# TensorE's identity products at three waits of each RWKV pair: loops of one product instead of products written out

## The reference

```python
def rwkv_mixer(pa, s0, w0, w_up, a0, a_up, g_up, k_k, k_a, r_k, gn_g, gn_b):
    ...
    r, k, v, wlo, alo, glo = jnp.split(pa, idx, axis=-1)
    kkf = heads((k * k_k).astype(jnp.float32))
    kk = kkf * lax.rsqrt(jnp.sum(kkf * kkf, axis=-1, keepdims=True) + 1e-12)
    g = jax.nn.sigmoid(glo) @ g_up
    for d, rev in enumerate((False, True)):
        w_log = -jax.nn.softplus(-(w0[d] + jnp.tanh(wlo) @ w_up[d]).astype(jnp.float32)) - 0.5
        decay = jnp.exp(-jnp.exp(w_log))
        a = jax.nn.sigmoid(a0[d] + alo @ a_up[d])
        kd = k * (1 + (a - 1) * k_a)
        y, s_fin = rwkv_scan(heads(r), heads(decay), heads(kd), heads(v), kk, heads(a), s0[:, d], rev)
    ...
```

## Time and profile before

| | |
|---|---|
| median of 3 runs | 3560.22 us (3550.71 to 3563.60) |
| the profiled execution, its own time | 3554.39 us |
| its span from first to last instruction | 3552.7 us |
| TensorE busy, share of the span | 3312.4 us, 93% |
| stage `rwkv` in the span | about 99 to 917 us |
| granted TensorE clock over the span | 0.981 of full speed |

### The profile page before, as it was taken

How to read it: one execution, slowest core, us unless ns; L and a number is a source line. 1 busy time by engine, 2 the same in 40 slices (tenths; PEclk the granted TensorE clock), 3 DMA queues, 4 the chain that set the end, 5 groups by cost and what they waited for, 6 DMA issues and landing times.

```text
span 3552.7 us, 155850 instructions
## 1 busy us (share of the span) xinstructions
PE 3312.4 (93%) x72354; PEld 2871.3 (81%) x72354; DVE 2133.6 (60%) x3890; ACT 765.1 (22%) x1815; POOL 388.7 (11%) x536
## 2 busy tenths in 40 slices
PE   7989899898999999299999999999999999999998
PEld 3575767767455545299999999999999999999997
DVE  4566667575344434666666666666666666666665
ACT  3434344444244443000000000000000000000002
POOL 0141524334211000000000000000000000000001
PEclk9999999999999999699999999999999999999999
DMA  8200000000311113399898898999889989898996
GB/s 358 73 5 9 18 10 17 5 20 5 99 33 33 44 54 107 128 325 286 284 290 278 290 285 281 286 291 287 283 287 288 284 282 292 284 289 287 283 288 211
DMA packets 570775, 671.20 MB, mean 189 GB/s; under 512 B 56942, under 2 KB 463750, under 8 KB 567054
## 3 DMA queue, kind: packets, MB, share of 16 engines
q1 hardware_dynamic: 564430, 641.85, 55.5%
q0 software_dynamic: 5520, 19.34, 2.4%
q10 hardware_dynamic: 176, 0.05, 0.0%
HBM read 631.68 MB, written 28.30 MB: 186 GB/s over the span
## 4 chain that ended last, share of the span: by engine, by line
PE 56%; issue 1%; SPq 1%; DVE 0%; DMA 0%; ACT 0%; DVEq 0%
PE banks L2515 34%; PE banks L2540 21%; PE banks L2456 2%; SPq L2363 1%; SPq L2370 0%; DMA e_wgu<-in_e_up 0%; DVE e_wgu L2819 0%; SPq L2373 0%; DVE e_wgu L2888 0%; DVE e_xe L2877 0%; DVE e_wsum L2717 0%; ACT e_xp L2655 0%; ACT e_xT L2655 0%; DVE e_wgu L2722 0%; DVE e_hid L2769 0%
## 5 line engine op out<-in xcount | busy, mean ns | idle before, releaser
L2540 PE MATMUL banks<-e_hid,e_wd 128*64 128x144 f32 x11264 | 1242.0, 287 | 6.7 <-issue 3.8
L2540 PEld LDWEIGHTS banks<-e_hid,e_wd 128*64 128x64 f32 x11264 | 744.4, 137 | 8.3 <-issue 8.2
L2515 PE MATMUL banks<-e_xsum,e_wsum 128*64 128x72 f32 x11264 | 514.3, 226 | 10.5 <-issue 7.8
L2515 PE MATMUL banks<-e_xT,e_wgu 128*64 128x72 f32 x11264 | 511.7, 226 | 12.6 <-issue 10.3
L2515 PE MATMUL banks<-e_xsum,e_wgu 128*64 128x72 f32 x11264 | 510.9, 226 | 7.9 <-issue 7.8
L2515 PEld LDWEIGHTS banks<-e_xsum,e_wsum 128*64 128x64 f32 x11264 | 492.7, 137 | 13.8 <-issue 11.0
L2515 PEld LDWEIGHTS banks<-e_xT,e_wgu 128*64 128x64 f32 x11264 | 491.4, 137 | 15.1 <-issue 14.8
L2515 PEld LDWEIGHTS banks<-e_xsum,e_wgu 128*64 128x64 f32 x11264 | 489.5, 137 | 10.1 <-issue 10.0
L2750 DVE TENSOR_TENSOR e_gu<-e_first,banks 128x288 f32<-128x288 f32 x176 | 79.9, 454 | 673.7 <-ACT e_first L2636 515.6
L2636 ACT ACTIVATE e_first<-banks 128x144 f32<-128x144 f32 x176 | 51.3, 291 | 1414.2 <-PE banks L2515 1414.2
L2515 PE MATMUL banks<-e_xT,e_wsum 128*64 128x72 f32 x5632 | 252.8, 226 | 2.8 <-issue 2.7
(11 more groups left out here) (401 smaller groups left out, 4754.3 us busy)
## 6 DMA issues: line engine op xcount, KB each, us to landing
e_wgu<-in_e_gate SPq DMA_DIRECT2D x704, 256.0 KB
e_wgu<-in_e_up SPq DMA_DIRECT2D x704, 256.0 KB
e_wd<-in_e_down SPq DMA_DIRECT2D x704, 256.0 KB, 4.0
h_wmod<-in_w_mod SPq DMA_DIRECT2D x24, 1024.0 KB, 16.5
wblk<-in_w_in SPq DMA_DIRECT2D x22, 512.0 KB, 21.6
h_x<-in_x_sample SPq DMA_DIRECT2D x8, 512.0 KB, 7.0
wo<-in_w_out SPq DMA_DIRECT2D x2, 2048.0 KB, 12.0
scratch_ffn<-hT_x SPq DMA_DIRECT2D x8, 512.0 KB, 5.2
```

Of the source, the lines that this page charges most:

```text
L2515: last = nc.tensor.matmul(bank[4 + 2 * (n % 2) + g][c, q * HT:(q + 1) * HT], a[:, k, c], b[:, k, :], start=(k == 0), stop=(k == HALF - 1))
L2540: last = nc.tensor.matmul(bank[k // PER_BANK][c, at:at + TOK], wd[n % WD][:, b, k * P + h * CH:k * P + (h + 1) * CH], hid[n % 2][:, b, :], ...
```

## The change

The function that issues the unused products becomes a loop of TensorE alone, whose body is one product. The number of products at each place stays 12, 9 and 16.

```diff
 def keep_warm(K, bank, n):
-    for _ in range(n):
+    with K.nc.Fori(0, n, engines=[mybir.EngineType.PE]):
         K.nc.tensor.matmul(K.bank[bank][:, 0:P], K.ident[:, :], K.ident[:, :], start=True, stop=True)
```

## The result

Over 20 runs of each kernel the median went from 3552.85 to 3561.36 us. The ratio is 1.0025 with a 95% interval of 1.0014 to 1.0036: 5 to 13 us slower, 9 in the middle. The 20 runs of before put its median 7 us under that of the first three, from which the prediction started. The profiled execution after took 3551.5 us, less than that of before (3554.4 us): the last stage alone, which the change leaves as it was, took 2063 us in place of 2073. So single executions can't be set against each other as a whole, and I read the places.

What follows compares the result with a forecast made beforehand. It took TensorE to be what the program waits for at the end of each group of unused products. 10.6 us lost at the third waits less 1.0 for blocks, on a 3560.2 median, gave 3570 us; range 3554 to 3600.

Steps and rivals of the forecast that it cites:

- The price of a turn: TensorE's sequencer, each loop turn: 0.03 us product, 0.1 addition, 0.20 compare-and-branch, 0.07 going back, 0.40 us in all.
- The first two waits: Groups of 12 and 9 products: sequencer far enough ahead to cover turns up to 0.8 and 0.47 us; cost none.
- cover of 9.9 us: First wait: 7.13 us of projection records plus 2.77 us of products on the array hide the 12 turns.
- The third wait: 16 products ahead of `v_major`: turns set the pace, 16 x (0.40 - 0.235) = 2.64 us a pair, 10.6 us in four.
- the lead: Third wait: sequencer may gain up to 0.3 us on the array while it works on L730; left out.
- The 1.0 us for fewer blocks: Instruction queue: 508 fewer instructions, two blocks less; at 0.52 us for each block's end, 1.0 us back.
- The sum: Whole kernel: 10.6 us lost less 1.0 us regained, 9.6 us later.
- Hidden: Rival, all three waits: a turn costs at most 0.235 us, unnoticed by the array; 0 to -1 us; chance 0.17.
- A dear turn: Rival, mainly third wait: a turn of 0.51 us costs 17.6 us, of 0.7 us 30 to 38 us; chance 0.22.
- Code fetched at each turn: Rival, all three waits: a fetch makes a turn 1.5 us; 37.5 us a pair, 150 us in all; chance 0.08.
- Faster: Rival: shorter code moves the 0.52 us stops under other waits in all pairs; 20 us gained, 3540 us; chance 0.03.
- The clock: Rival, behind each loop: spread-out products drop the granted clock to 0.50; 13.6 us more, 3583 us; chance 0.02.

Runs made afterwards that it cites:

- fewer-products run: 9, 7 and 15 unused products written out, without loops, in place of 12, 9 and 16 of the kernel before; ratio 1.0012 (0.9997 to 1.0027).

## Why the prediction was right, and where its sizes were off

**The mechanism and the place** were those forecast: the sequencer's price of a turn, at the third wait alone. The run with a loop at the third wait alone has the whole loss, and the run with loops at the other two has none.

**The price of a turn** was put at 0.40 us and is 0.39 in the median, with one of 0.42 to 0.48 in every six or so. From the first addition to the first product of `v_major` the 16 turns of pair 0 take 6.35 us, 0.40 each. The parts come out as well, which is in part luck, for they were taken from rows of other instructions, and the 0.07 from none. The branch starts 0.10 us behind the addition, as was put, though the addition's own duration is 36 ns. From the branch to the next addition it is 0.29 us, of which 208 ns are the branch's own; 0.30 was put (0.20, 0.07 for going back, 0.03 for the product). The product adds nothing that shows. The Trainium skill, page "Advanced Engine Details and Errata", section "Control Flow Timing", gives about 108 ns for a compare-and-branch. The trace differs: 208 ns when it goes back, 76 when it falls through. By the page the third group would have kept its length; it grew by 2 us.

**The first two waits** were to cost nothing, for the sequencer is ahead there. They cost nothing, and it enters the first loop 7 us early. But the prediction's cover of 9.9 us for the first wait is not how it works. While the array is on L606, the additions start 0.86 us apart, a turn for each two records of L606, and in each pair eight products have been handed over when the array begins the first. The lead is thus some eight products here, though 7 us of L606 stand ahead; the last turns, at 0.38 us, are hidden behind those eight. By these numbers, an estimate, 8 x 0.22 us of lead at 0.39 - 0.22 us lost a turn is used up after some ten further turns, so a loop of more than about 18 products would show at this place too.

**The third wait** was to lose 2.64 us a pair and lost 1.9 to 2.1. The term that was mis-sized is the lead, put at "up to 0.3 us" and left out. The first addition starts 0.52 us ahead of the array's first product in pair 0 and 0.66 or 0.67 in the others, for the sequencer goes on to the loop while the array works on L730: 2.5 us in four pairs. So the products' starts are 0.22 us apart for the first few, behind a first distance of 0.33, and then 0.39. 10.6 less 2.5 is the 8.0 that was measured.

**The 1.0 us for fewer blocks** was too large and did not appear. Two blocks less are there, and the stops are at blocks' ends, as was supposed; but only 59 of 135 ends stop TensorE, so two ends are worth 2 x 30.8 / 135 = 0.5 us by the trace of before. The issue waits differ by 4 us between two executions of one kernel, so the term is below what can be seen, and the fewer-products run shows that the place of a block's end can cost more than the number of blocks saves.

**The sum** of 9.6 stands against 8.0 in the trace's third waits and 9 by the ratio, 5 to 13. That it lies so near is in part luck, for the lead left out made it 2.5 us too large and the term for blocks up to 1.0 too small. The 3570 us lie 9 above the 3561.4 measured, nearly all of it because the first three runs of before were high. The prediction also held that less than 0.5% can't be told from no change; 20 runs of each kernel do tell this 0.25% from none.

**The rivals.** Hidden: out, by the run with a loop at the third wait alone. A dear turn: out, at 0.39. Code fetched at each turn: out; the queue moved 566 blocks, and a turn would have taken over 1.1 us. The Trainium skill, page "Runtime: NRT & Kernel Launch", section "Instruction fetch mechanics", limits the fetch to targets outside the pages at hand, and the trace agrees for these short bodies. Faster: did not happen. The clock: 1.00 at the third wait and for 124 us behind it, with the products 0.39 us apart.

## What to carry to other kernels

A loop of TensorE is paid on its sequencer, beside the array. Ask at each place how far the sequencer is ahead: behind long instructions 9 or 12 turns of 0.39 us vanish, right behind a wait that holds the sequencer the turn is the pace. Ask too how long the lead lasts; here it was some eight products. Where the body is shorter than a turn, put enough into it to cover the turn (here two products of 0.22 us), or count the turns by time and not by the products they replace.

## What the runs showed that was not expected

The unused products matter more than how they are written: without them the kernel is 20 us slower, 0.56%, and a wait of 1.94 us at the first place was followed by a clock of 0.50. And code that is only moved can stop TensorE: in the fewer-products kernel `v_major`, 288 instructions that otherwise take 2.3 us, stood still for 1.3 to 1.6 us near its end in two pairs of four, in both executions, where an ordinary stop in the main part is 0.5 us. It did so where two ends of blocks of 256 instructions fell into it. A gain of 3.4 us was lost to it.
